# Set-up of a state-space layer: loads reordered, B transposed on TensorE, kernel blocks spread in 2 KB pieces from one queue

## The chip, the cores and the metric

The kernel runs on one core of one Trainium2 chip. A core has TensorE (PE, matrix products and transposes), VectorE (DVE), ScalarE (ACT), GpSimd (POOL) and SyncE (SP, which here only issues DMA transfers), a shared on-chip memory of 128 partitions (SBUF) and an accumulator memory of eight banks (PSUM: ACC has four, SS two, MI two). Engines run on their own and meet at semaphores. The metric is the device time of one execution in microseconds, the median of several.

## The reference

One step of a two-layer decoder over a prompt of 512 tokens and 8 x 4 sample tokens, all in float32. The change lies in the first mixer:

```python
y, h = s5_ssm(rmsnorm(h), ...)      # 64 groups of 16 channels, one 64-dim complex state each
# inside: dt = exp(log_dt); A = exp((lam_re + i lam_im) dt)
#         B' = f(A, lam) * B;  h_t = A h_{t-1} + B' u_t;  y_t = Re(C h_t) + D u_t
gl = gelu(y) @ w_glu + b_glu        # then ConvFFN, embedding gate, attention layer, ConvFFN ...
```

## The kernel before

Nearly all of the time goes to streamed weights: strips of 128 columns of every weight matrix are loaded by SP into RAW, split by GpSimd into two parts (L616, L618) and multiplied by PE (L831). Ahead of the first strip stands the state-space layer, some 200 us, and the change is all in there.

The scan runs in chunks of CH = 8 positions, for 32 pairs of groups. Its set-up, by engine:

- SP (from L426) issues small loads: constants, lam, log_dt, the gain row G2; then B (L439, two transfers straight into BC in the order needed, 64 bytes a piece), C (L443, 16 transfers), vectors, states, convolution parameters. ACT's queue loads x at once (L1239 to L1245).
- PE turns lam and log_dt (L676), makes the gain row in SS (L679), turns C into ACC (L683, `c_made`), turns x by eighths through the two banks of MI (L694), then vectors, convolution parameters, states, and the scaled x (`uz_made`).
- DVE computes the powers of A from log_dt (L1700 to L1816, `a_ready`, `powers_in`), multiplies B by the gains (L1822), builds the powers A^j B for both halves of the pairs (L1843 to L1851, `pc_ready`), makes the diagonal DG (L1855), then the squarings for the rotation table (L1859, "levels", 30 small instructions), the table EROT (L1870), and then one scan for each f of 8 (L1887).
- GpSimd multiplies C by powers in `powers(0)`, as soon as `a_ready` and `c_turned` are there, and `powers(1)` after `uz_made`. Each runs eight half-cycles of two L585 and one L588, on 1, 2, 4 and 1 positions.
- ACT copies C (`c_turned`), squares x (L1255), takes the root (L1258), copies x out of PSUM (L1262), scales it (L1279) and copies results of PE.

The local part of y is a block-Toeplitz product. `kernels(h)` on PE makes its 8 blocks of 16 rows for half h of the pairs, ACT copies them into KKE behind seven blocks of zeros (L1312), and then SP "spreads" them: 64 transfers for each half, one for each of 8 row blocks j and 8 groups b, copy KKE shifted by j blocks into KT (L486), semaphore `kt_in0` or `kt_in1`. PE's `outputs(f)` reads KT (L788); outputs(0) to (3) need the first half, outputs(4) to (7) the second. In PE's program the order is inputs(f + 1), turn_z(f - 1), kernels(1) at f = 1, outputs(f). After both halves SP loads the first weight strip (L491).

Of the kernel before, what the change touches and what calls it, by code (L numbers as in the profile page):

```python
# [18 lines left out]
F32 = mybir.dt.float32  # L19
# [112 lines left out]
def build(nc, x_prompt, x_sample, state_ssm_re, state_ssm_im, state_ffn_conv, cache_k_win, cache_v_win,  # L132
# [5 lines left out]
    with ExitStack() as ctx:  # L138
# [79 lines left out]
        early = Region(n_at + 2 * PAIRS * CH * CG * 4)  # L218
        TAB = early("TAB", [P, 2, 1024])

        KKE = early("KKE", [P, KC // 2, (2 * CH - 1) * CG])
        SSQ = early("SSQ", [P, CH])
        RST = early("RST", [P, CH])
        MSK = early("MSK", [P, CG])
# [13 lines left out]

        Z = nc.alloc_sbuf_tensor_at("Z", [P, KC, 2, NTOK], F32R, offset=perm.at)
        XS = nc.alloc_sbuf_tensor_at("XS", [P, CH, D], F32, offset=perm.at)  # L240
        KT = nc.alloc_sbuf_tensor_at("KT", [P, NBL, P], F32, offset=perm.at + 2048)

        BD = nc.alloc_sbuf_tensor_at("BD", [P, 2, PAIRS, 2 * CG], F32, offset=perm.at + 2048 + NBL * P * 2)
        ph1 = Region(perm.at + 2 * KC * NTOK * 4)
        uz_at = ph1.at
        UZ = ph1("UZ", [P, NBL, NC_])
# [19 lines left out]
        LD2 = stg("LD2", [2, PAIRS])  # L266
        SEL = stg("SEL", [2, P])
        G2 = stg("G2", [2, PAIRS * CG])
        SQJ = stg("SQJ", [P, D])
        assert stg.at <= uz_at + NBL * NC_ * 4  # L270

# [154 lines left out]
        def _(sp):  # L426
            LOAD = [sem("load0"), sem("load1")]

            with nc.allow_non_contiguous_dma(reason="64 small elements"):
# [5 lines left out]
                sp.dma_start(LD2[:], ssm_log_dt[0].rearrange("(q a) -> a q", a=2)).then_inc(sem("lam_in"), 16)  # L435
                sp.dma_start(G2[:].rearrange("a (q c) -> a q c", c=CG),
                             g_mix[0].rearrange("(q a c) -> a q c", a=2, c=CG)).then_inc(sem("g_in"), 16)
            for r, src in enumerate((ssm_b_re, ssm_b_im)):
                sp.dma_start(BC[:, r], src[0].rearrange("(q a) s c -> (a s) q c", a=2)).then_inc(sem("b_in"), 16)  # L439
            for r, src in enumerate((ssm_c_re, ssm_c_im)):  # L440
                for t in range(4):
                    for a in range(2):
                        sp.dma_start(CS_[:, r, t, 64 * a:64 * a + 64],  # L443
                                     src[0].rearrange("(t q a) c s -> t a q c s", t=4, a=2)[t, a]).then_inc(sem("c_in"), 16)
            for at0, src in ((V_GMIX, g_mix), (V_GFFN, g_ffn), (V_GPLE, g_ple)):
                sp.dma_start(VECS[at0:at0 + 16, :], src.rearrange("l (c p) -> (l c) p", p=P)).then_inc(sem("vec_in"), 16)
            sp.dma_start(VECS[V_GKV:V_GKV + 8, :], g_kv.rearrange("(c p) -> c p", p=P)).then_inc(sem("vec_in"), 16)
# [19 lines left out]
            def stream(name, parts, begin=0):  # L467

                def turn(i, free):
                    for u in range(2):  # L470
                        if free:

                            sp.wait_ge(sem("split_done"), i * 2 + (strip_of(name, u) - 1))
                        todo = parts(i, u)
                        for dst, src in todo:
                            sp.dma_start(dst, src).then_inc(LOAD[u], 64 // len(todo))

                n = dict(order)[name] // 2
                if name == "glu":

                    for h in range(2):
                        sp.wait_ge(sem("uz_made"), len(XG))
                        sp.wait_ge(sem("kk_ready"), h + 1)
                        for j in range(CH):
                            for b in range(8):
                                sp.dma_start(KT[CG * j:CG * j + CG, NBL // 2 * h:NBL // 2 * h + NBL // 2, :].rearrange(  # L486
                                    "p (f b) n -> p f b n", b=8)[:, :, b, :],
                                    KKE[CG * b:CG * b + CG, :, CG * (CH - 1 - j):CG * (CH - 1 - j) + P]).then_inc(sem("kt_in%d" % h), 16)

                    sp.wait_ge(sem("kt_in1"), 16 * CH * 8)  # L490
# [66 lines left out]
        def _(pool):  # L557
# [11 lines left out]
            PIN.memset(TIC[:], 0.0).then_inc(sem("ones_set"), 1)  # L569

            pool.wait_ge(sem("ones_set"), 1)
            PIN.memset(KKE[:, :, 0:(CH - 1) * CG], 0.0).then_inc(sem("kz_set"), 1)
            pool.wait_ge(sem("kz_set"), 1)

            def powers(h):
# [90 lines left out]
        def _(pe):  # L666
# [14 lines left out]
            for r in range(2):  # L681
                for t in range(4):
                    last = turn(ACC[:, r, P * t:P * t + P], CS_[:, r, t, :], P)  # L683
                last.then_inc(sem("c_made"), 1)

            pe.wait_ge(sem("x_in"), 112)
            pe.wait_ge(sem("xz_set"), 1)
            pe.wait_ge(sem("xs_zero"), 1)
            for m in range(KC):
                for jh in range(2):  # L690
                    if m:
                        pe.wait_ge(sem("x_turned"), 2 * m + jh - 1)
                    for j in range(4):
                        last = turn(MI[:, jh, NC_ * j:NC_ * j + NC_], XS[0:NC_, 4 * jh + j, P * m:P * m + P], NC_)  # L694
                    last.then_inc(sem("x_made"), 1)
            pe.wait_ge(sem("vec_in"), 160)
            pe.wait_ge(sem("c_turned"), 2)
            turn(ACC[:, 0, 0:V_N], VECS[:], V_N).then_inc(sem("vec_made"), 1)
            pe.wait_ge(sem("cp_in"), 128)
            for t in range(4):  # L700
# [74 lines left out]
            def outputs(f):  # L775


                par = f % 2
                pe.wait_ge(sem("kt_in%d" % (f // 4)), 16 * CH * 8)
                if f:  # L780
                    pe.wait_ge(sem("y_taken"), f)
                else:
                    pe.wait_ge(sem("kk_taken"), 1)
                pe.wait_ge(sem("h0_placed"), f + 1)
                pe.wait_ge(sem("h_ready"), f + 1)
                for q in range(FQ):
                    for a in range(2):
                        mm(SS[0:NU_, a, P * q:P * q + P], UZ[:, 8 * f + 2 * q + a, 0:NU_], KT[:, 8 * f + 2 * q + a, :],  # L788
                           start=True, stop=False, skip_group_check=True)
                    for r in range(2):  # L790
                        for a in range(2):
                            rows = slice(64 * a, 64 * a + 64)
                            last = mm(SS[0:NU_, a, P * q:P * q + P], HSV[rows, par, r, q, 0:NU_],  # L793
                                      CA[rows, r, FQ * f + q, 1:CH + 1, :].rearrange("p t c -> p (t c)"),
                                      start=False, stop=r == 1, skip_group_check=True)
                last.then_inc(sem("y_made"), 1)
# [401 lines left out]
        def _(act):  # L1198
# [60 lines left out]
            for m in range(KC):  # L1259
                for jh in range(2):  # L1260
                    act.wait_ge(sem("x_made"), 2 * m + jh + 1)
                    src = MI[:, jh, 0:4 * NC_].rearrange("p (j c) -> p j c", c=NC_)  # L1262
# [43 lines left out]
            def kernels(h, src):  # L1306
# [5 lines left out]
                copy(KKE[:, :, (CH - 1) * CG:], src.rearrange("p (f n) -> p f n", n=P)).then_inc(sem("kk_taken"), 1)  # L1312
# [364 lines left out]
        def _(dve):  # L1677
# [181 lines left out]
            for lv in range(6):  # L1859
                t = TURNS + 3 * lv  # L1860
                w = A4_RE + 2 if lv == 0 else t - 3
                T(PR[:, X4:X4 + 2, :], PR[:, w:w + 2, :], PR[:, w:w + 2, :], M_)
                link(T(pr(X6), pr(w), pr(w + 1), M_))
                T(pr(t), pr(X4), pr(X5), S_)
                T(pr(t + 2), pr(X4), pr(X5), S_)
                link(T(pr(t + 1), pr(X6), pr(X6), A_))
# [377 lines left out]
```

## Time and profile before

| | |
|---|---|
| median of 3 runs | 1491.46 us (1490.61 to 1493.36) |
| profiled execution, its own time | 1493.79 us |
| its span | 1491.9 us |
| PE busy | 1347.7 us, 90% |
| GpSimd busy | 773.2 us, 52% |
| DVE busy | 752.4 us, 50% |
| ACT busy | 441.6 us, 30% |

```profile
PE   0463769999999999999999998899999999999998
...
PEclk9995779999999999999999999999999999999999
DMA  7011115322222233333355312132332223332322
```

Each of the 40 digits stands for a fortieth of the span, 37.3 us: the busy share in tenths for PE and the DMA engines, the granted TensorE clock in tenths of full speed between them. The first six slices are the set-up; after them PE is busy without a break.

### The profile page before, as it was taken

The page shows a single profiled execution, that of the slowest core. Times are in us where ns is not written, and L with a number is a line of the kernel's source. Part 1 is how long each engine was busy: PE and PEld are TensorE (multiplying, and loading weights), DVE is VectorE, ACT ScalarE, POOL GpSimd, SP SyncE. Part 2 cuts the span into 40 slices and gives each one's busy share as a digit, 9 for nine tenths or more (in the row PEclk, how much of TensorE's full clock was granted, in tenths as well). Part 3 has the DMA queues.
Part 4 walks back from the last instruction along what each step waited for, and adds up shares of the span by engine and source line. Part 5 has one row for each costly group of instructions (what it writes and reads, how often), then busy time and mean ns, then how long its engine had stood idle before and what let it go on. Part 6 is the DMA issues. An engine that isn't in the chain of part 4 may idle for free.

```text
span 1491.9 us, 28737 instructions
## 1 busy us (share of the span) xinstructions
PE 1347.7 (90%) x10924; PEld 1295.5 (87%) x10924; DVE 752.4 (50%) x1310; ACT 441.6 (30%) x941; POOL 773.2 (52%) x669
## 2 busy tenths in 40 slices
PE   0463769999999999999999998899999999999998
PEld 0452548999999999999999985699999999999998
DVE  4886633225555555213376876555555555312253
ACT  0751212113343333111124137423334333210021
POOL 1770005655665556556565545455566655656552
PEclk9995779999999999999999999999999999999999
DMA  7011115322222233333355312132332223332322
GB/s 95 13 22 36 41 47 115 87 84 84 86 84 84 87 93 98 86 91 89 98 113 133 94 43 79 31 95 71 91 92 84 84 84 91 106 90 81 91 86 63
DMA packets 237799, 120.19 MB, mean 81 GB/s; under 512 B 34413, under 2 KB 236992, under 8 KB 237420
## 3 DMA queue, kind: packets, MB, share of 16 engines
q1 hardware_dynamic: 227640, 107.06, 26.1%
q10 hardware_dynamic: 10092, 12.20, 3.9%
q8 instruction: 47, 0.77, 0.2%
q14 instruction: 20, 0.16, 0.0%
HBM read 110.98 MB, written 6.09 MB: 78 GB/s over the span
## 4 chain that ended last, share of the span: by engine, by line
PE 82%; SPq 7%; ACT 4%; DVE 3%; issue 2%; POOL 1%; ACTq 0%; DMA 0%; DVEq 0%; POOLq 0%
PE ACC L831 55%; PE MI L831 10%; PE SS L831 8%; SPq L486 5%; PE MI L671 4%; SPq L439 1%; PE SS L788 1%; PE SS L793 1%; SPq L443 1%; ACT PB L1630 1%; ACT XN L1202 1%; PE SS L1016 1%; PE SS L1138 1%; DVE PB L2173 1%; DVE RSTD L1971 0%
## 5 line engine op out<-in xcount | busy, mean ns | idle before, releaser
L618 POOL TENSOR_TENSOR SPL<-RAW,SPL 128x1024 fp32r<-128x1024 f32 (+2 forms) x172 | 449.6, 2614 | 14.3
L831 PE MATMUL ACC<-NH,SPL 128*128 128x272 f32 x2048 | 350.1, 289 | 0.7 <-DVE AL L2032 0.7
L615 POOL TENSOR_TENSOR TIC<-EPSB 128x1 f32<-128x1 f32 x172 | 37.0, 215 | 597.0 <-PE ACC L831 343.6
L831 PEld LDWEIGHTS ACC<-NH,SPL 128*128 128x128 f32 x2048 | 291.5, 189 | 1.8 <-issue 0.9
L831 PE MATMUL ACC<-AH,SPL 128*128 128x272 f32 x1408 | 237.6, 289 | 0.0
L831 PE MATMUL ACC<-NL,SPL 128*128 128x272 f32 x1024 | 211.3, 288 | 0.0
L831 PEld LDWEIGHTS ACC<-AH,SPL 128*128 128x128 f32 x1408 | 198.9, 188 | 0.2
L616 POOL TENSOR_SCALAR SPL<-RAW 128x1024 fp32r<-128x1024 f32 (+2 forms) x172 | 195.2, 1135 | 0.0
L831 PEld LDWEIGHTS ACC<-NL,SPL 128*128 128x128 f32 x1024 | 160.9, 189 | 0.0
L831 PE MATMUL ACC<-AL,SPL 128*128 128x272 f32 x704 | 145.4, 287 | 0.0
L831 PE MATMUL SS<-NH,SPL 128*128 128x272 f32 x704 | 120.6, 288 | 0.0
L831 PE MATMUL MI<-NH,SPL 128*128 128x272 f32 x704 | 120.6, 288 | 0.0
L1685 DVE SCALAR_TENSOR_TENSOR ACC<-WK,CP,ACC 128x560 f32<-128x560 f32 x88 | 70.9, 805 | 95.7 <-ACT ACC L1202 89.3
L831 PEld LDWEIGHTS ACC<-AL,SPL 128*128 128x128 f32 x704 | 111.0, 188 | 0.0
L2047 DVE TENSOR_TENSOR H<-ACC,H 128x544 f32 (+1 forms) x24 | 17.4, 724 | 183.4 <-PE ACC L831 183.2
L1685 DVE SCALAR_TENSOR_TENSOR NL<-H,VEC,NH (+1 forms) x40 | 80.3, 2016 | 47.7 <-ACT NH L1489 29.7
L831 PE MATMUL ACC<-Z,SPL 128*128 128x272 f32 x768 | 100.0, 292 | 3.2 <-ACT WK L1401 2.3
L831 PEld LDWEIGHTS ACC<-Z,SPL 128*128 128x128 f32 x768 | 98.3, 191 | 4.5 <-issue 3.3
L831 PEld LDWEIGHTS MI<-NH,SPL 128*128 128x128 f32 x704 | 100.5, 189 | 0.0
L831 PEld LDWEIGHTS SS<-NH,SPL 128*128 128x128 f32 x704 | 100.5, 189 | 0.0
L831 PE MATMUL ACC<-XQH,SPL 128*128 128x272 f32 x512 | 90.1, 294 | 0.9 <-DVE XQL L1685 0.9
L831 PEld LDWEIGHTS ACC<-XQH,SPL 128*128 128x128 f32 x512 | 74.4, 191 | 1.9 <-DVE XQL L1685 1.1
(329 smaller groups left out, 2006.2 us busy)
## 6 DMA issues: line engine op xcount, KB each, us to landing
RAW<-in_w_up_dram SPq DMA_DIRECT2D x88, 512.0 KB
RAW<-in_w_down_dram SPq DMA_DIRECT2D x32, 704.0 KB
RAW<-in_w_glu_dram SPq DMA_DIRECT2D x16, 512.0 KB
RAW<-in_w_ple_gate_dram SPq DMA_DIRECT2D x16, 512.0 KB
KT<-KKE SPq DMA_DIRECT2D x128, 32.0 KB, 2.0
RAW<-in_w_q_dram SPq DMA_DIRECT2D x16, 256.0 KB
RAW<-in_w_o_dram SPq DMA_DIRECT2D x32, 128.0 KB
RAW<-in_w_ple_in_dram SPq DMA_DIRECT2D x16, 128.0 KB
```

The lines of the kernel that those rows point to most:

```text
L439: sp.dma_start(BC[:, r], src[0].rearrange("(q a) s c -> (a s) q c", a=2)).then_inc(sem("b_in"), 16)
L443: sp.dma_start(CS_[:, r, t, 64 * a:64 * a + 64], src[0].rearrange("(t q a) c s -> t a q c s", t=4, a=2)[t, a]).then_inc(sem("c_in"), 16)
L486: sp.dma_start(KT[CG * j:CG * j + CG, NBL // 2 * h:NBL // 2 * h + NBL // 2, :].rearrange("p (f b) n -> p f b n", b=8)[:, :, b, :], KKE[CG ...
L615: PIN.tensor_tensor(TIC[:], EPSB[:], EPSB[:], ALU.add)
L616: PIN.tensor_scalar(hi, RAW[:, u, 0:kt, :], 1.0, 1.0, ALU.mult, ALU.mult).then_inc(sem("high_done"), 1)
L618: PIN.tensor_tensor(lo, RAW[:, u, 0:kt, :], hi.bitcast(F32), ALU.subtract).then_inc(sem("split_done"), 1)
L671: return tr(out, in_, IDN[0:rows, 0:rows])
L788: mm(SS[0:NU_, a, P * q:P * q + P], UZ[:, 8 * f + 2 * q + a, 0:NU_], KT[:, 8 * f + 2 * q + a, :], start=True, stop=False, skip_group_check ...
L793: last = mm(SS[0:NU_, a, P * q:P * q + P], HSV[rows, par, r, q, 0:NU_], CA[rows, r, FQ * f + q, 1:CH + 1, :].rearrange("p t c -> p (t c)") ...
L831: last = mm(out[:, h, :], SPL[:, u, w, w0 + k, :], x[:, k0 + k, HT * h:HT * h + HT], start=start and k == 0 and n == 0, stop=stop and k == ...
L1685: return nc.vector.scalar_tensor_tensor(out=out, in0=in0, scalar=scalar, in1=in1, op0=op0, op1=op1)
L2047: T(halves(H[:, i * 2 + u, :]), acc(u), halves(H[:, i * 2 + u, :]), A_).then_inc(sem(norm + "_h"), 1)
```

## The change

The C loads go ahead of the B loads. B comes in its natural order, 8 KB a row, and PE turns it (32 transposes) into ACC; ACT copies the gain row from PSUM to GS first, and DVE's multiplication reads these two. ACT waits for lam and log_dt before it issues the x loads. x is turned through four banks instead of two, and vectors, convolution parameters and states are turned after the last of x is copied. DVE's level loop moves from behind DG to before the multiplication of B. KKE and KT are laid out with the tap (position) outermost, so that one transfer copies 16 rows of 2 KB, contiguous on both sides; there are 128 transfers as before and all are on SP's queue. KT becomes two tensors; the second lies where the first half of PC lies, so SP waits for `v_made` of 4 before it spreads the second half.

```diff
-        KKE = early("KKE", [P, KC // 2, (2 * CH - 1) * CG])
+        KKE = early("KKE", [P, 2 * CH - 1, KC // 2, CG])
...
-        KT = nc.alloc_sbuf_tensor_at("KT", [P, NBL, P], F32, offset=perm.at + 2048)
+        KT = [nc.alloc_sbuf_tensor_at("KT%d" % h, [P, 8, CH, KC // 2, CG], F32, offset=o) for h, o in
+              ((0, perm.at + KC * NTOK * 4), (1, n_at))]
+        BN = nc.alloc_sbuf_tensor_at("BN", [PAIRS, 2, P, CG], F32, offset=n_at)
...
+        XB = (MI[:, 0], MI[:, 1], ACC[:, 0], ACC[:, 1])
+        def spread(h, j, b):
+            return (KT[h][CG * j:CG * j + CG, b].rearrange("p i f c -> p (i f c)"),
+                    KKE[CG * b:CG * b + CG, CH - 1 - j:2 * CH - 1 - j].rearrange("p t f c -> p (t f c)"))
...
-            for r, src in enumerate((ssm_b_re, ssm_b_im)):
-                sp.dma_start(BC[:, r], src[0].rearrange("(q a) s c -> (a s) q c", a=2)).then_inc(sem("b_in"), 16)
             for r, src in enumerate((ssm_c_re, ssm_c_im)):
...
+            for r, src in enumerate((ssm_b_re, ssm_b_im)):
+                sp.dma_start(BN[:, r], src[0].rearrange("(q a) s c -> q (a s) c", a=2)).then_inc(sem("b_in"), 16)
...
                         sp.wait_ge(sem("kk_ready"), h + 1)
+                        if h:
+                            sp.wait_ge(sem("v_made"), KC // 2)
                         for j in range(CH):
                             for b in range(8):
-                                sp.dma_start(KT[CG * j:CG * j + CG, NBL // 2 * h:NBL // 2 * h + NBL // 2, :].rearrange(
-                                    "p (f b) n -> p f b n", b=8)[:, :, b, :],
-                                    KKE[CG * b:CG * b + CG, :, CG * (CH - 1 - j):CG * (CH - 1 - j) + P]).then_inc(sem("kt_in%d" % h), 16)
+                                sp.dma_start(*spread(h, j, b)).then_inc(sem("kt_in%d" % h), 16)
...
+            pe.wait_ge(sem("b_in"), 32)
+            for r in range(2):
+                for c in range(CG):
+                    last = tr(ACC[:, 2 + r, PAIRS * c:PAIRS * c + PAIRS], BN[:, r, :, c], IDN[0:PAIRS, 0:PAIRS])
+            last.then_inc(sem("b_made"), 1)
...
-                    if m:
-                        pe.wait_ge(sem("x_turned"), 2 * m + jh - 1)
+                    if m >= 2:
+                        pe.wait_ge(sem("x_turned"), 2 * m + jh - 3)
...
-            pe.wait_ge(sem("c_turned"), 2)
+            pe.wait_ge(sem("x_turned"), 2 * KC)
             turn(ACC[:, 0, 0:V_N], VECS[:], V_N).then_inc(sem("vec_made"), 1)
...
-                        mm(SS[0:NU_, a, P * q:P * q + P], UZ[:, 8 * f + 2 * q + a, 0:NU_], KT[:, 8 * f + 2 * q + a, :],
+                        mm(SS[0:NU_, a, P * q:P * q + P], UZ[:, 8 * f + 2 * q + a, 0:NU_], KT[f // 4][:, 2 * q + a, :, f % 4, :],
...
+            act.wait_ge(sem("lam_in"), 48)
             for i in range(4):
                 act.dma_start(XS[NSEQ:64, 2 * i:2 * i + 2, :], chunks[0:64 - NSEQ, 2 * i:2 * i + 2, :]).then_inc(sem("x_in"), 16)
...
+            act.wait_ge(sem("g_made"), 1)
+            copy(GS[:], SS[:, 1, :]).then_inc(sem("g_copied"), 1)
...
-            dve.wait_ge(sem("g_made"), 1)
-            dve.wait_ge(sem("b_in"), 32)
+
+            for lv in range(6):
+                t = TURNS + 3 * lv
...
+            dve.wait_ge(sem("g_copied"), 1)
+            dve.wait_ge(sem("b_made"), 1)
             for r in range(2):
-                last = T(BC[:, r].rearrange("p q c -> p (q c)"), BC[:, r].rearrange("p q c -> p (q c)"), SS[:, 1, :], M_)
+                last = T(BC[:, r], ACC[:, 2 + r, :].rearrange("p (c q) -> p q c", q=PAIRS), GS[:].rearrange("p (q c) -> p q c", c=CG), M_)
```

## Rows read from the trace of the kernel before

**Rows 1.** The page's chain that ended last, shares by engine

```profile
PE 82%; SPq 7%; ACT 4%; DVE 3%; issue 2%; POOL 1%; ACTq 0%; DMA 0%; DVEq 0%; POOLq 0%
```

**Rows 2.** Chain in order of time, 0 to 260 us: start, us, what

```profile
4.26 19.23 SPq L439
```

**Rows 3.** Source line L486, SP: ns min/median/max, first and last start

```profile
L486 SPq DMA_DIRECT2D KT<-KKE x128: 585/595/1572, 95.3 to 197.2; - x128
...
DMA to landing us min/median/max: 2.0/2.0/3.1
```

**Rows 4.** Timeline 0 to 60 us: start, us, engine, line, operation [idle before]

```profile
2.95 0.32 SPq L435 DMA_DIRECT2D LD<-in_ssm_log_dt_dram  x1
...
23.04 0.34 PE L671 MATMUL SS<-IDN,LAMS 64*128 64x64 f32 x1 [23.04 <-DMA LD<-in_ssm_log_dt_dram]
...
38.62 0.35 DVE L1816 COPY SS<-PR 128x192 f32<-128x192 f32 x1
...
39.01 1.28 DVE L1822 TENSOR_TENSOR BC<-BC,SS 128x512 f32<-128x512 f32 x2
...
39.55 1.05 ACT L1255 ACTIVATE ZTK<-XS 80x1024 f32<-80x1024 f32 x1
...
49.73 0.20 DVE L1845 RECIPROCAL RST<-RST 80x8 f32<-80x8 f32 x1 [5.33 <-ACT RST L1258]
```

**Rows 5.** Timeline 57 to 100 us

```profile
76.33 1.22 DVE L1834 TENSOR_TENSOR PC<-TE,ACC 128x1024 f32<-128x1024 f32 x1
...
83.12 0.29 DVE L1857 TENSOR_TENSOR DG<-MSK,DGV 128x128 f32<-128x128 f32 x1
...
87.95 0.65 PEld L751 LDWEIGHTS SS<-CA,BD 128*32 128x32 f32 x16 [0.33 <-issue]
...
94.36 0.60 ACT L1202 ACTIVATE KKE<-SS 128x512 f32<-128x512 f32 x1 [5.70 <-PE SS L754]
...
95.28 5.29 SPq L486 DMA_DIRECT2D KT<-KKE  x8
```

**Rows 6.** Timeline 57 to 170 us, DVE beside GpSimd

```profile
93.92 1.32 POOL L588 TENSOR_TENSOR CA<-TAB 128x512 f32<-128x512 f32 x1
...
94.03 1.26 DVE L1865 TENSOR_TENSOR PR<-PR 128x32 f32<-128x32 f32 x1
...
95.33 3.76 POOL L585 TENSOR_TENSOR TAB<-CA,PR 128x1024 f32<-128x1024 f32 x2
...
99.17 2.41 POOL L588 TENSOR_TENSOR CA<-TAB 128x1024 f32<-128x1024 f32 x1
...
101.83 0.09 DVE L1868 MEMSET EROT<- 128x32 f32 x1
```

**Rows 7.** DMA queues, 7-8 and 18-19 us: packets, MB, engine share

```profile
q10 hardware_dynamic: 28, 0.19, 87.0%
...
q1 hardware_dynamic: 98, 0.01, 60.7%
```

**Rows 8.** Issues by source line: ns min/median/max; timeline on SP

```profile
L539 SPq DMA_DIRECT2D RAW<-in_w_o_dram x8: 596/617/718, 868.8 to 877.8; - x8
...
37.50 0.32 SPq L449 DMA_DIRECT2D VECS<-in_b_glu_dram  x1
...
37.86 0.56 SPq L452 DMA_DIRECT2D VECS<-in_k_norm_dram  x2
```

**Rows 9.** Timeline 100 to 262 us

```profile
124.42 0.08 DVE L1883 MEMSET HSV<- 128x8 f32 x2
...
138.52 1.12 PE L788 MATMUL SS<-KT,UZ 128*72 128x128 f32 x4 [10.38 <-DMA KT<-KKE]
...
154.20 0.60 ACT L1202 ACTIVATE KKE<-ACC 128x512 f32<-128x512 f32 x1 [4.53 <-PE ACC L754]
...
161.55 1.22 PE L770 MATMUL ACC<-UZ,PC 128*64 128x72 f32 x32
...
199.22 1.13 PE L788 MATMUL SS<-KT,UZ 128*72 128x128 f32 x4 [22.46 <-DMA KT<-KKE]
```

More of the change, by code:

```diff
@@ L240, in build @@
         XS = nc.alloc_sbuf_tensor_at("XS", [P, CH, D], F32, offset=perm.at)
-        KT = nc.alloc_sbuf_tensor_at("KT", [P, NBL, P], F32, offset=perm.at + 2048)
-        BD = nc.alloc_sbuf_tensor_at("BD", [P, 2, PAIRS, 2 * CG], F32, offset=perm.at + 2048 + NBL * P * 2)
+        KT = [nc.alloc_sbuf_tensor_at("KT%d" % h, [P, 8, CH, KC // 2, CG], F32, offset=o) for h, o in
+              ((0, perm.at + KC * NTOK * 4), (1, n_at))]
+        BD = nc.alloc_sbuf_tensor_at("BD", [P, 2, PAIRS, 2 * CG], F32, offset=perm.at + KC * NTOK * 4 - 8192)
+        BN = nc.alloc_sbuf_tensor_at("BN", [PAIRS, 2, P, CG], F32, offset=n_at)
         ph1 = Region(perm.at + 2 * KC * NTOK * 4)
@@ L268, in build @@
         G2 = stg("G2", [2, PAIRS * CG])
+        GS = stg("GS", [P, PAIRS * CG])
         SQJ = stg("SQJ", [P, D])
@@ L571, in _ @@
             pool.wait_ge(sem("ones_set"), 1)
-            PIN.memset(KKE[:, :, 0:(CH - 1) * CG], 0.0).then_inc(sem("kz_set"), 1)
+            PIN.memset(KKE[:, 0:CH - 1], 0.0).then_inc(sem("kz_set"), 1)
             pool.wait_ge(sem("kz_set"), 1)
@@ L688, in _ @@
             pe.wait_ge(sem("xs_zero"), 1)
+            pe.wait_ge(sem("c_turned"), 2)
             for m in range(KC):
                 for jh in range(2):
-                    if m:
-                        pe.wait_ge(sem("x_turned"), 2 * m + jh - 1)
+                    if m >= 2:
+                        pe.wait_ge(sem("x_turned"), 2 * m + jh - 3)
                     for j in range(4):
-                        last = turn(MI[:, jh, NC_ * j:NC_ * j + NC_], XS[0:NC_, 4 * jh + j, P * m:P * m + P], NC_)
+                        last = turn(XB[2 * (m % 2) + jh][:, NC_ * j:NC_ * j + NC_], XS[0:NC_, 4 * jh + j, P * m:P * m + P], NC_)
                     last.then_inc(sem("x_made"), 1)
             pe.wait_ge(sem("vec_in"), 160)
-            pe.wait_ge(sem("c_turned"), 2)
+            pe.wait_ge(sem("x_turned"), 2 * KC)
             turn(ACC[:, 0, 0:V_N], VECS[:], V_N).then_inc(sem("vec_made"), 1)
@@ L1261, in _ @@
                     act.wait_ge(sem("x_made"), 2 * m + jh + 1)
-                    src = MI[:, jh, 0:4 * NC_].rearrange("p (j c) -> p j c", c=NC_)
+                    src = XB[2 * (m % 2) + jh][:, 0:4 * NC_].rearrange("p (j c) -> p j c", c=NC_)
                     if jh == 0:
@@ L1311, in kernels @@
                 act.wait_ge(sem("kz_set"), 1)
-                copy(KKE[:, :, (CH - 1) * CG:], src.rearrange("p (f n) -> p f n", n=P)).then_inc(sem("kk_taken"), 1)
+                copy(KKE[:, CH - 1:].rearrange("p t f c -> p f t c"), src.rearrange("p (f t c) -> p f t c", f=KC // 2, c=CG)).then_inc(sem("kk_taken"), 1)
                 act.wait_ge(sem("kk_taken"), h + 1)
@@ L1818, in _ @@
             dve.wait_ge(sem("powers_in"), 1)
-            dve.wait_ge(sem("g_made"), 1)
-            dve.wait_ge(sem("b_in"), 32)
+            for lv in range(6):
+                t = TURNS + 3 * lv
+                w = A4_RE + 2 if lv == 0 else t - 3
+                T(PR[:, X4:X4 + 2, :], PR[:, w:w + 2, :], PR[:, w:w + 2, :], M_)
+                link(T(pr(X6), pr(w), pr(w + 1), M_))
+                T(pr(t), pr(X4), pr(X5), S_)
+                T(pr(t + 2), pr(X4), pr(X5), S_)
+                link(T(pr(t + 1), pr(X6), pr(X6), A_))
+            dve.wait_ge(sem("g_copied"), 1)
+            dve.wait_ge(sem("b_made"), 1)
             for r in range(2):
-                last = T(BC[:, r].rearrange("p q c -> p (q c)"), BC[:, r].rearrange("p q c -> p (q c)"), SS[:, 1, :], M_)
+                last = T(BC[:, r], ACC[:, 2 + r, :].rearrange("p (c q) -> p q c", q=PAIRS), GS[:].rearrange("p (q c) -> p q c", c=CG), M_)
             link(last)
@@ L1857, in _ @@
             T(DG[:], MSK[:].unsqueeze(1).to_broadcast([P, KC, CG]), DGV[:].unsqueeze(2).to_broadcast([P, KC, CG]), M_).then_inc(sem("dg_ready"), 1)
[L1859 to L1866, printed above, removed]
             dve.wait_ge(sem("uz_made"), len(XG))
```

## The prediction

> **What bounds the kernel now.** The page's chain by engine comes first: TensorE holds 82% of it, SyncE's queue 7% [rows 1]. The 7% is where this change acts. The chain in order of time puts it in two places: a 19.2 us issue of the second B load at 4.26 [rows 2], and the "spreading" transfers. There are 128 of them, median 0.595 us to issue, 2.0 us to land [rows 3]. Before the weight strips can stream, the kernel is a chain of set-up, and its steps are these. PE starts at 23.04 on log_dt, issued at 2.95; DVE computes the powers, done at 38.97 (38.62 + 0.35), 15.9 us later; ACT squares x from 39.55; DVE idles 5.33 us for the root at 49.73 [rows 4]. DVE ends the B powers at 77.55, makes DG at 83.12, PE starts kernels(0) at 87.95, ACT copies it at 94.36, SP spreads from 95.28 [rows 5]. PE's outputs(0) starts at 138.52 when the last transfer lands, and outputs(4) at 199.22 after a 22.46 us wait for the second half [rows 9]. Everything behind outputs(4) only shifts with it: the work from there on is unchanged.
>
> **Loads and log_dt.** The change holds the x loads until lam_in. Where is log_dt then? Before, the x queue filled 87% of the DMA engines (7 to 8 us), and even at 18 to 19 us SP's queue moved 98 packets in 60.7% of 16 engine-us, 99 ns a packet [rows 7]. Alone, log_dt's 64 four-byte pieces cost 3 to 6 us at that price. Issue end 3.27, plus 2.0 to land, plus 3.0: 8.3. Bounds are 5.3 (pieces free) and 23.0 (x had no part in it); I take 8.3, as the queue ahead of it holds only small loads. Powers then end at 24.2.
>
> The Trainium skill ("DMA: Bandwidth & Descriptors", on why a DMA increments its semaphore by 16) says that a transfer from SP or ACT uses the largest number of engines up to 16 that divides the slowest dimension of both sides. For log_dt that is 2, so 32 pieces each: an estimate of 3.2 us at the row's 99 ns, landing at 8.5; on one engine 6.3 us and 11.6. No row shows single engines; either would shift the sum by at most 3 us.
>
> x then lands at about 24.6 (before, x ran some 16.3 us from its first issue: the x queue's packets end by 17 us in the DMA view) plus up to 5 for C and B beside it; I take 27.5. ACT starts squaring there instead of 39.55, 12 us sooner. The x transposes through four banks are worth some 2 us, the vec, conv and state transposes now queued behind them cost 1. So the ACT/PE chain would reach kernels(0) 13 us sooner, at 75. B in 8 KB rows frees SP of the 19.2 us issue; its 32 PE transposes (under 0.2 us each) and one ACT copy lie inside that wait for x.
>
> **The moved level loop.** DVE's 30 instructions for the rotation levels move from after DG to before B is multiplied. In the old place they were slow: a step of DVE on 32 columns ends with the step of GpSimd beside it, L1865 at 94.03 + 1.26 = 95.29 and POOL L588 at 93.92 + 1.32 = 95.24. So levels advance one per GpSimd half-cycle (two L585, one L588): from DG's end at 83.41 to 101.83 it is 18.4 us [rows 5, 6], of which the first level, before GpSimd started, 0.8. Six levels at that 0.8 are some 5 us. In the new place GpSimd's powers(0) starts as soon as C is turned. C is now first in the queue, and I put C turned at 19 to 29, centre 23. That is beside the loop at 24.2. The five levels that met GpSimd took 17.6; a sixth meets a second half-cycle of the longest kind, 3.76 + 2.41 = 6.2 [rows 6]. That is 24 us, so B is multiplied at 48.3, not 29: nine later than before. From there to the end of the B powers is 77.55 - 39.01 - 5.33 (the wait for the root is gone by then) = 33.2 [rows 4, 5], giving 81.5. DG 0.5 more. kernels(0) needs DG and DVE works in order: it starts at 82.1 instead of 75. Net against before: **-5.8 us**. Bounds: -13 (no collision) and 0.
>
> The Trainium skill ("SBUF — State Buffer", section "SBUF: two separate sides") speaks against this move: a VectorE instruction with two SBUF inputs and a GpSimd instruction that reads SBUF exclude each other for whole instructions, while one with a PSUM input does not contend. The trace agrees, 1.26 beside 1.32 us. By that rule the whole loop costs 24 us if powers(0) runs through it; without it the sum is that of the first rival below.
>
> The rotation table (101.8 to 124.4, 22.6 us [rows 6, 9]) then starts at 82.1, beside powers(1); 24 us, and the first scan 5.7 us: 112. That is below the next figure, so it is hidden. If the spread were 4 us shorter still, it would be next.
>
> **Spreading.** Before: 95.28 to 138.52 is 43.2 us = 64 x 0.644 + 2.0; second half, from about 155.1 (ACT's copy into KKE at 154.20 plus 0.9) to 199.22, 44.1 = 64 x 0.658 + 2.0 [rows 5, 9]. Each transfer was 64 pieces of 512 B, a stepped pattern on both sides. It becomes 16 contiguous pieces of 2 KB. Price of such an issue: nearest is b_glu, 16 rows against 16 rows, 0.316 us, next issue 0.36 after it. Against it stands 0.617 for w_o's issues, whose pattern is stepped again [rows 8]. I take 0.33 + 0.05 = 0.38, since the plain two-level pattern is what b_glu has. Then a half is 64 x 0.38 + 2.0 = 26.3: **-16.9** and **-17.8**. Bounds 0.30 and 0.67 per transfer. The transferred bytes stay; DMA is no limit.
>
> **The new wait.** SP now waits before the second half until inputs(3) is done on PE, as KT[1] lies on PC. PE finished it at 161.55 + 1.22 = 162.8, SP had started at 155.1: **+7.7** [rows 9]. Behind the wait on SP are only the 64 transfers and then the first glu strips. PE's outputs(1) to (3) run meanwhile. The strided KT operand (64 B runs) and the strided KKE copy (0.60 us, twice) I take at nothing, as the same columns pass. The bounds: four L788 took 1.12 us [rows 9], and 96 of the 128 lie on the path (outputs 2 and 3 do not), so a fifth more each is 5 us, double 27.
>
> **Sum.** -5.8 - 16.9 + 7.7 - 17.8 = -32.8. In steps: SP starts at 89.4, outputs(0) at 115.7, second spread at 140.0, outputs(4) at 166.4 instead of 199.2. Against the profiled execution, 1493.8 us with a span of 1491.9, that is 1461.0; it lies 2.3 over the median of 1491.46, so the median becomes 1458.7.
>
> **Rivals.**
> (a) No collision: C lands late enough, or log_dt early enough, that the levels end first. kernels(0) at 75, sum -13 - 34.7 + 7.7 = -40.0: 1451.5. For it: x fills the engines while C lands. Against: C is issued first.
> (b) log_dt stays late at 23.0, by its own small pieces: powers at 38.9, plus 24 + 33.2 + 0.6 puts kernels(0) at 96.7, +8.7. Sum -18.3: 1473.2. For it: 99 ns packets with x gone.
> (c) Slower: an issue costs by transfer, not by piece. W_o's issues took as long as the spreading ones with other pieces. At 0.617 + 0.05 each of the 128 costs 0.667 against 0.651: nothing comes back, +2.0, and the new wait's 7.7 outweighs the 5.8: +3.9, 1495.4. It decides from about 0.636 per transfer.
> (d) The strided operand slows PE by a fifth: 1464.
>
> **Numbers.** Main 0.48, own range 1451 to 1470; (a), with partial collisions, 0.24; (b) 0.14; (c) 0.07; (d) and others 0.07. The range of 8 in 10 reaches 1444 to 1477. A measurement tells about 0.2%, 3 us, from nothing. Faster 0.90, same 0.04, slower 0.06.
>
> **What would show it.** PE's first matmul near 8 us; ACT L1255's counterpart near 27; the level loop 20 us or more long with GpSimd busy beside it; DVE and not PE late for kernels(0); issues of 0.33; SP idle some 8 us for v_made after the second kernels; outputs(4) near 166. An issue of 0.59 makes the prediction wrong by itself; so does a first matmul at 20.

## The result, and the profile after

The changed kernel takes 1489.4 us (median of 16, 1485.8 to 1491.6) beside 1492.2 (16 runs, 1489.7 to 1496.6) for the kernel before: ratio 0.9974, interval 0.9963 to 0.9984. It is faster by 0.16 to 0.37%, where 2.2% were forecast, and lies outside the range. The profiled execution, 1488.0 us with a span of 1486.0, is 5.9 below the span before; the medians differ by 2.8, so of the last 3 us of any accounting here nothing is sure. Each variant below was run beside the kernel before. Where two variants are compared, both the difference of the medians and that of the two ratios are given if they disagree.

The steps of the prediction, in us on the profiled timelines:

| step | before | predicted | after |
|---|---|---|---|
| PE starts on log_dt | 23.04 | 8.3 | 4.89 |
| powers done on DVE | 38.97 | 24.2 | 20.84 |
| six levels take | (behind DG) 18.4 | 24 | 4.7 |
| ACT squares x | 39.55 | 27.5 | 31.73 |
| DG | 83.12 | 81.5 | 73.21 |
| kernels(0) | 87.95 | 82.1 | 78.05 |
| SP spreads, first half | 95.28 | 89.4 | 83.42 |
| outputs(0) | 138.52 | 115.7 | 126.69 |
| SP spreads, second half | 155.10 | 140.0 | 150.76 |
| outputs(4) | 199.22 | 166.4 | 193.20 |

The page's chain by engine has hardly moved; SyncE's queue still has its 7% [rows 1]:

```profile
PE 83%; SPq 7%; ACT 4%; DVE 3%; issue 2%; POOL 1%; ACTq 0%; DMA 0%; DVEq 0%; POOLq 0%
```

The source line of the spreading transfers says why: with 2 KB pieces in place of 512 B ones, the issue has the price that it had [rows 3], and so has the landing.

```profile
L498 SPq DMA_DIRECT2D KT<-KKE x128: 507/589/1702, 83.4 to 191.2; - x128
...
DMA to landing us min/median/max: 1.9/2.0/3.1
```

The timeline of the changed kernel from 0 to 40 us (start, us, engine, line, operation) shows the loads. PE's wait for log_dt ends at 4.89. DVE runs the first level at 20.87 and ends the sixth at 25.57, while GpSimd is idle until 31.53. PE waits 21.11 us for the last C load and turns C; ACT copies it out before it squares x [rows 4]:

```profile
4.89 0.34 PE L681 MATMUL SS<-IDN,LAMS 64*128 64x64 f32 x1 [4.89 <-DMA LD<-in_ssm_log_dt_dram]
...
9.12 17.95 SPq L451 DMA_DIRECT2D CSTG<-in_ssm_c_im_dram  x8
...
20.49 0.35 DVE L1837 COPY SS<-PR 128x192 f32<-128x192 f32 x1
20.87 0.22 DVE L1844 TENSOR_TENSOR PR<-PR 128x64 f32<-128x64 f32 x1
...
25.39 0.18 DVE L1848 TENSOR_TENSOR PR<-PR 128x32 f32<-128x32 f32 x1
...
28.76 1.97 PE L681 MATMUL ACC<-IDN,CSTG 128*128 128x128 f32 x8 [21.11 <-DMA CSTG<-in_ssm_c_im_dram]
...
31.53 1.20 POOL L595 TENSOR_TENSOR TAB<-CA,PR 128x256 f32<-128x256 f32 x2 [25.36 <-ACT CA L1219]
31.73 1.05 ACT L1276 ACTIVATE ZTK<-XS 80x1024 f32<-80x1024 f32 x1
...
35.51 1.29 DVE L1852 TENSOR_TENSOR BC<-ACC,GS 128x512 f32<-128x512 f32 x2 [9.94 <-PE ACC L699]
```

Farther on the same timeline (60 to 200 us): kernels(0) at 78.05, whose first group runs at 1.10 us for 16 matmuls and the other three at 0.67, where all four took 1.10 before; the two bursts; outputs(0) and outputs(4) held by the transfers [rows 5, 9].

```profile
73.21 0.29 DVE L1887 TENSOR_TENSOR DG<-MSK,DGV 128x128 f32<-128x128 f32 x1
...
78.05 1.10 PE L768 MATMUL SS<-CA,BD 128*32 128x128 f32 x16
79.62 0.67 PE L768 MATMUL SS<-CA,BD 128*32 128x128 f32 x16
...
82.50 0.60 ACT L1219 ACTIVATE KKE<-SS 128x512 f32<-128x512 f32 x1 [3.75 <-PE SS L771]
83.42 6.96 SPq L498 DMA_DIRECT2D KT<-KKE  x11
...
126.69 1.12 PE L805 MATMUL SS<-KT,UZ 128*72 128x128 f32 x4 [25.59 <-DMA KT<-KKE]
...
142.42 0.60 ACT L1219 ACTIVATE KKE<-ACC 128x512 f32<-128x512 f32 x1 [4.89 <-PE ACC L771]
143.05 0.20 ACT L1335 ACTIVATE TIC<-EPSB 128x1 f32<-128x1 f32 x1
149.44 1.22 PE L787 MATMUL ACC<-UZ,PC 128*64 128x72 f32 x32
150.76 14.50 SPq L498 DMA_DIRECT2D KT<-KKE  x22
...
193.20 1.13 PE L805 MATMUL SS<-KT,UZ 128*72 128x128 f32 x4 [28.55 <-DMA KT<-KKE]
```

So: -11.9 at the first spreading start, nothing in the first burst (43.27 against 43.24), +7.5 for the new wait (143.25, when ACT's signal is out, to 150.76), -1.7 in the second burst (42.44 against 44.12). Before rounding the sum is -6.0, which is outputs(4)'s shift (199.22 to 193.20); the span's is 5.9. From outputs(4) to the end all profiled kernels take the same time, 1292.0 to 1294.6 us.

The faster groups of kernels(0), 2.0 of the 11.9, can't be put down to the change. Two of the kernels below, both with few transfers, are the same program up to that point. One ran its last groups at 0.67 and the other at 1.10 (timelines of 80 to 160 us, the first line from the run with eight loads a half, the second from the one with the store early):

```profile
81.29 0.67 PE L771 MATMUL SS<-CA,BD 128*32 128x128 f32 x16
...
82.47 1.10 PE L771 MATMUL SS<-CA,BD 128*32 128x128 f32 x16
```

So this pace can differ between executions of the same instructions. The granted clock doesn't explain it here: from 80 to 83 us it reads 1.00 in the changed kernel, whose groups run at 0.67, and 1.00 in the variant with the levels behind DG, whose groups run at 1.10. Why is open.

### The profile page after: what moved, and what is told of

It reads as the page before. It is cut to its first block, busy times and chain, and to the rows that moved or that the text cites. A ratio compares the mean times of both kernels' runs of the same rounds, so it can differ in the third digit from the quotient of the medians.

```text
span 1486.0 us, 28802 instructions
## 1 busy us (share of the span) xinstructions
PE 1346.1 (91%) x10956; PEld 1295.6 (87%) x10956; DVE 746.7 (50%) x1310; ACT 441.7 (30%) x942; POOL 780.0 (52%) x669
## 4 chain that ended last, share of the span: by engine, by line
PE 83%; SPq 7%; ACT 4%; DVE 3%; issue 2%; POOL 1%; ACTq 0%; DMA 0%; DVEq 0%; POOLq 0%
PE ACC L848 55%; PE MI L848 10%; PE SS L848 8%; SPq L498 5%; PE MI L681 3%; SPq L451 1%; PE SS L810 1%; PE SS L805 1%; ACT PB L1651 1%; ACT XN L1219 1%; PE SS L1033 1%; PE ACC L681 1%; PE SS L1155 1%; DVE PB L2194 1%; DVE RSTD L1992 0%
## 5 line engine op out<-in xcount | busy, mean ns | idle before, releaser
L628 POOL TENSOR_TENSOR SPL<-RAW,SPL 128x1024 fp32r<-128x1024 f32 (+2 forms) x172 | 449.8, 2615 | 14.4
```

Of the source, the lines that this page charges most:

```text
L628: PIN.tensor_tensor(lo, RAW[:, u, 0:kt, :], hi.bitcast(F32), ALU.subtract).then_inc(sem("split_done"), 1)
```

## Experiments

**Prices of single transfers.** SP's queue issues bursts of 24 transfers of different kinds between two SBUF buffers or DRAM, each burst alone.

```
+ sp.dma_start(B[16 partitions, 512 floats], A[16 partitions, 512 floats])       # L45
+ sp.dma_start(B[16 partitions, 4 x 128 floats], A[16 partitions, 4 x 128 floats, stepped])   # L50: 4 pieces of 512 B a row
+ sp.dma_start(B[...], src[16:32, 512 floats])   # L55: DRAM to SBUF
+ sp.dma_start(spare[...], A[...])               # L60: SBUF to DRAM
+ 1 x 2 KB (L75); 16 x 64 B (L80); 16 rows of 16 KB (L95); two queues at once (L100 on SP, L110 on ACT)
```

> This kernel computes nothing of the reference: SP issues bursts of 24 transfers of one form each, and waits for the landings between bursts. It asks what the 0.59 us that each spreading transfer keeps SP (before and after the change) hangs on. Theory A, a price by transfer whatever it carries, in a long burst: every burst shows a median of 0.59, the 1-row, 4-row, 8-row, 16 x 64 B and 128 x 2 KB ones too. Theory B, the price of the on-chip source with on-chip destination: 0.59 in the SBUF to SBUF bursts, 0.30 to 0.40 in the bursts of 16 x 2 KB from or to DRAM. Theory C, by pieces or bytes: 1 row and 16 x 64 B well under 0.4, 128 rows above 0.59. Theory D, by the stepped pattern, on which my prediction stood: 4 x 512 B a row 0.59, 2 KB a row 0.33; the changed kernel's trace speaks against it already. The last burst runs on SP and ACT at once: if both keep 0.59 a second queue doubles the rate; if each goes to 1.2 the two share one generator.

Measured (source line views: ns min/median/max, first and last start):

```profile
L45 SPq DMA_DIRECT2D B<-A x24: 563/589/590, 18.0 to 32.5; - x24
...
L50 SPq DMA_DIRECT2D B<-A x24: 594/595/672, 34.4 to 49.2; - x24
...
L55 SPq DMA_DIRECT2D B<-in_src_dram x24: 403/420/423, 51.2 to 61.8; - x24
...
L60 SPq DMA_DIRECT2D spare<-A x24: 302/420/478, 63.6 to 74.5; - x24
...
L75 SPq DMA_DIRECT2D B<-A x24: 583/589/590, 110.0 to 124.5; - x24
...
L80 SPq DMA_DIRECT2D B<-A x24: 531/589/591, 126.2 to 140.7; - x24
...
L95 SPq DMA_DIRECT2D B<-A x8: 572/2518/2691, 164.7 to 178.2; - x8
...
L100 SPq DMA_DIRECT2D B<-A x24: 507/590/607, 187.5 to 202.1; - x24
...
L110 ACTq DMA_DIRECT2D C<-A x24: 555/611/766, 187.6 to 202.4; - x24
```

A transfer from SBUF to SBUF costs 0.589 us to issue whether it is one piece of 2 KB, 16 of 2 KB or 16 of 64 B. With four pieces of 512 B a row, the form that the change replaced, it costs 0.595. With DRAM on either side, 16 plain rows cost 0.42. So the pieces were not what cost, and b_glu's 0.316, which the prediction took, is a load from DRAM. Even that was no price for a burst: the 24 DRAM loads of L55 start 0.46 us apart. The ends are not the whole rule either, as a DRAM load can cost as much by its shape: the median stepped C load of the changed kernel takes 0.589, and w_o's 0.617 [rows 8]. Two queues at once keep their rate: 48 transfers in 15.4 us.

**The loads and the levels alone.** The changed kernel with the old KKE and KT layout, 512 B pieces and no wait for v_made.

```
- sp.wait_ge(sem("v_made"), KC // 2)
- sp.dma_start(*spread(h, j, b))
+ sp.dma_start(KT[CG*j:CG*j+CG, ...][:, :, b, :], KKE[CG*b:CG*b+CG, :, CG*(CH-1-j):CG*(CH-1-j)+P])
```

> The changed kernel with KT, KKE, the spreading transfers and the missing v_made wait of the kernel before: the load order, B on TensorE and the moved level loop alone. My theory (the loads gave 11.9 us at the start of the first spread, the wait took 7.5 back, the pieces nothing): spread starts near 83.4, outputs(0) near 126.7, second spread right after kk_ready near 143, outputs(4) near 187; time 11 to 13 us under before, 0.992 of it, and 5 to 7 under the changed kernel. Rival (2 KB pieces do help somewhere, in landing or contention): not faster than the changed kernel, 0.997.

Measured 1483.75 us, ratio 0.9942 (0.9929 to 0.9956). The spread starts at 83.39, outputs(0) at 126.97, and the second half's transfers at 143.50, as soon as ACT's signal is out. Outputs(4) starts 5.5 before the changed kernel's (timeline of 110 to 200 us):

```profile
187.68 1.13 PE L803 MATMUL SS<-KT,UZ 128*72 128x128 f32 x4 [23.03 <-DMA KT<-KKE]
```

By its ratio this half of the change is worth 8.6 us (6.6 to 10.6). The steps came as expected and the time did not: 11 to 13 were forecast, from a timeline that had the 2.0 of kernels(0)'s faster groups in it.

**The pieces alone.** The kernel before with the new layout, 2 KB pieces and the wait, the loads and the levels as they were.

```
- KKE = early("KKE", [P, KC // 2, (2 * CH - 1) * CG])
+ KKE = early("KKE", [P, 2 * CH - 1, KC // 2, CG])
+ if h: sp.wait_ge(sem("v_made"), KC // 2)
+ sp.dma_start(*spread(h, j, b))
```

> The kernel before with KT and KKE by tap, 2 KB pieces and the v_made wait, the loads and the level loop left as before. My theory: first spread 95.3 to 138 as before at 0.59 an issue, second held from 155 to 162.8, so 6 to 8 us slower than before: 1.004 to 1.005. Rival (the pieces help): same or faster than before. The strided KT operand would show as L788 above 0.28 us at the low clock and 0.16 at the high.

Measured 1499.49 us, ratio 1.005 (1.0036 to 1.0063): 7.5 slower (5.4 to 9.4), as the new wait's price would have it. (Its profiled execution is only 3.1 over the span before, as its spreading started at 92.24.) The two halves together, -8.6 and +7.5, give -1.1 against a measured -3.9 (-5.5 to -2.4), about what their intervals allow. The second burst takes 42.7 here (159.51 to 202.25), 42.4 in the changed kernel, and 44.1 to 44.2 in the two kernels with 512 B pieces. The first bursts differ by less, 42.9 and 43.3 against 43.2 and 43.6. So there may be 1 or 2 us in the pieces; as the second burst also starts behind another wait, no run separates the two.

**Few transfers.** KKE goes to device memory in one store and comes back in 8 loads of 256 KB a half.

```
+ sp.dma_start(kk_rows[h], KKE[:].rearrange("p t f c -> p (t f c)")).then_inc(sem("kd_out"), 16)
+ sp.wait_ge(sem("kd_out"), 16 * (h + 1))
  for j in range(CH):
-     for b in range(8):
-         sp.dma_start(*spread(h, j, b))
+     sp.dma_start(KT[h][CG*j:CG*j+CG].rearrange(...), kk_rows[h].rearrange("(b c) x -> c b x", b=8)[..., 64*(CH-1-j): +512])
```

> The changed kernel with the spreading of a half as one store of KKE to DRAM (480 KB), its landing, and 8 loads of 256 KB (16 rows by 8 pieces of 2 KB) in place of 64 transfers of 32 KB; bytes into KT unchanged. Theory 1, the number of issues is the wall: half lands some 17 us after its start instead of 43; outputs(0) then waits for DVE's first scan (about 110), outputs(4) near 151 instead of 193; time 36 to 44 us under before, 0.972. Theory 2, bytes or the writes of 16 rows are the wall (53 GB/s seen): nothing gained, and the round trip costs 3 to 6 us more than the changed kernel: 1.000.

Measured 1448.2 us (1445.8 to 1452.9), ratio 0.9707 (0.9683 to 0.9731): 41 us below the changed kernel by the medians, 40 by the ratios, and outputs(4) starts 38.8 earlier. Its timeline (80 to 160 us) has the store, the eight loads in 3.6 us, an outputs(0) that now waits for DVE's scan, and an outputs(4) that waits 7 us where it waited 28.6:

```profile
83.24 0.36 SPq L496 DMA_DIRECT2D kk_rows<-KKE  x1
...
85.80 3.63 SPq L499 DMA_DIRECT2D KT<-kk_rows  x8
...
109.41 1.10 PE L808 MATMUL SS<-KT,UZ 128*72 128x128 f32 x4 [8.85 <-DVE HSV L1934]
...
133.47 0.34 SPq L496 DMA_DIRECT2D kk_rows<-KKE  x1
...
154.40 1.13 PE L808 MATMUL SS<-KT,UZ 128*72 128x128 f32 x4 [7.04 <-DMA KT<-kk_rows]
```

The bytes and the pieces that go into KT are the same as in the changed kernel. What changed is the number of issues, 9 for 64, and that each now has one end in DRAM. This run doesn't separate the two. By an estimate, 64 issues 0.46 apart, as in the DRAM burst of the single prices, and 2.0 to land would be 31.4 us; the burst takes 43.3, and this run's second half 20.9 (133.47 to 154.40). So the ends alone could give 11.9 and leave 10.5 to the number. That it is SP's issuing and not the way between the two ends that fills the 43 us is shown by the next run, which leaves both ends in SBUF. What is left here is the transfers themselves: from 135 to 150 us the DMA engines are busy by 0.84 and more, where the spreading held them at 0.20 to 0.25. Still fewer issues should gain little; that was not run.

**Two queues.** The changed kernel, blocks 4 to 7 of the first half issued by ACT behind its KKE copy.

```
-     for b in range(8):                      # SP
+     for b in range(4 if h == 0 else 8):
...
+ act.wait_ge(sem("kk_ready"), 1)
+ act.wait_ge(sem("uz_made"), len(XG))
+ for j in range(CH):
+     for b in range(4, 8):
+         act.dma_start(*spread(0, j, b)).then_inc(sem("kt_in0"), 16)
```

> The changed kernel, but half of the first half's spreading (blocks 4 to 7 of each tap, 32 of the 64 transfers) is issued by ScalarE behind its copy of the kernels; the second half stays on SyncE. Theory 1 (the price of a spreading transfer is its issue on one queue, 0.64 us, and two queues don't share it, as in the run of single prices): the first half's transfers are out 0.64 x 32 = 20.5 us after the start instead of 41, so the first outputs matmul comes at about 107 to 110 instead of 126.7, bounded by VectorE's scan (ready near 109.8); v_made follows sooner by as much, the second burst starts near 135 instead of 150.8, the fifth outputs group near 177 instead of 193.2: 1489.4 - 16 = 1473 us (1468 to 1479). ScalarE is held for some 20 us, its turned copies of the next input groups come late by that, which is a cost that the idle 25 us of TensorE hide. Theory 2 (the price is paid in what both queues share: descriptor generation for a transfer with both ends on chip, or the 16 engines): both queues slow to about 1.2 us a transfer, the first outputs matmul stays at 126 or later, 1489 to 1495 us.

Measured 1471.8 us, ratio 0.9872 (0.9858 to 0.9886), 1.2 from the forecast. That is 17.6 below the changed kernel by the medians and 15.2 by the ratios; outputs(4) starts 14.4 earlier. The timeline of 80 to 120 us:

```profile
85.57 20.82 ACTq L1341 DMA_DIRECT2D KT<-KKE  x32
85.63 21.04 SPq L498 DMA_DIRECT2D KT<-KKE  x32
...
106.44 0.32 ACT L1219 ACTIVATE VSM<-ACC 128x32 f32<-128x32 f32 x2 [20.89 <-issue]
...
106.89 1.29 DVE L1922 TENSOR_TENSOR T<-ACC,EROT 128x512 f32<-128x512 f32 x2 [9.20 <-ACT VSM L1219]
```

Both queues issue at 0.65 us each side by side: half the transfers, half the time. Not all is as forecast: ACT, held for 20.9 us, copies the samples late, DVE's scan waits 9.2 for that, and outputs(0) starts at about 118, not at 107 to 110. Outputs(4) starts at 178.8 instead of 193.2. The Trainium skill ("DMA: Bandwidth & Descriptors", section "Issuing engines are not separate DMA queues") says that a second issuing engine saves only the time of initiating, "usually small relative to the DMA itself". The saving is as it says; it isn't small here: 0.65 of issue for each transfer in the queue against one landing of 2.0 at the end. The Trainium skill ("Perfetto Trace Analysis", section "DMA Instruction — HWDGE (DVE, Sync)") has one descriptor generator shared by two sequencers, each locking it for itself while its descriptors are made. If that took up most of an issue, the two bursts would take nearly twice as long; with 0.590 and 0.611 side by side against 0.589 alone, no run shows such a wait.

**The x loads not held.**

```
- act.wait_ge(sem("lam_in"), 48)
```

> The changed kernel, but ScalarE's loads of x do not wait for the lambda and log_dt loads to land. Theory 1 (the x transfers filling the engines are what kept log_dt at 23 us in the kernel before): log_dt lands late again, near 20 to 23 us instead of 4.9; powers and levels then end near 43 instead of 25.6; x lands some 4 us sooner and the C loads no later than 28.7; the B multiply that starts at 35.5 moves to 44 or later, so all up to the spreading start moves 6 to 10 us later (83.4 to 90 to 93): 1489.4 + 8 = 1497 us (1493 to 1501). Theory 2 (it is the loads' order on SyncE's queue and the missing B loads that let log_dt land early, the wait does nothing): within 1 us of the changed kernel, 1488 to 1491 us.

Measured 1507.1 us, ratio 1.0105 (1.0089 to 1.012): 17.7 above the changed kernel by the medians, 19.5 by the ratios: twice the forecast of 8. The direction holds, as PE gets log_dt only at 21.57. The size is the collision of the prediction, which comes true here. C is turned before the powers end, GpSimd's powers(0) runs, and the six levels take from 40.26 to 62.37, 22.1 us for 4.7. These are PE's first line (timeline of 0 to 45 us) and then DVE and GpSimd on the timeline of 36 to 64 us:

```profile
21.57 0.34 PE L681 MATMUL SS<-IDN,LAMS 64*128 64x64 f32 x1 [21.57 <-DMA LD<-in_ssm_log_dt_dram]
...
40.26 0.23 DVE L1843 TENSOR_TENSOR PR<-PR 128x64 f32<-128x64 f32 x1
40.37 2.05 POOL L595 TENSOR_TENSOR TAB<-CA,PR 128x512 f32<-128x512 f32 x2 [2.31 <-DVE SS L1836]
...
51.25 2.43 POOL L598 TENSOR_TENSOR CA<-TAB 128x1024 f32<-128x1024 f32 x1
51.26 0.23 DVE L1843 TENSOR_TENSOR PR<-PR 128x64 f32<-128x64 f32 x1
51.40 2.33 DVE L1844 TENSOR_TENSOR PR<-PR 128x32 f32<-128x32 f32 x1
...
62.40 1.29 DVE L1851 TENSOR_TENSOR BC<-ACC,GS 128x512 f32<-128x512 f32 x2
```

The step of 2.33 beside GpSimd's 2.43 takes 0.18 alone. Spreading starts at 104.3 instead of 83.4.

**The levels behind DG again.** The rest as in the changed kernel.

```
- for lv in range(6): ...        # ahead of the B multiply
+ for lv in range(6): ...        # the same five instructions each, behind DG
```

> The changed kernel, but the loop of six levels stands again behind the gather of DG on VectorE. Theory 1 (the levels fall in idle time of VectorE at 20.9 to 25.6 us, 4.7 us in all, so moving them gained nothing for the spreading's start, and behind DG they delay only the rotation tables, whose scan is done 17 us before the first outputs matmul needs it): spreading starts at 83.4 as in the changed kernel, the levels collide with GpSimd and take 12 to 25 us there, the first scan is ready at 122 to 135 instead of 109.8; the first outputs matmul waits for the spread (126.7) or for the scan up to 8 us beyond: 1489.4 to 1497 us, forecast 1491. Theory 2 (the early levels are what let the first kernels come sooner, since something on their way reads them): spreading starts later than 86 and the time goes to 1493 or more by the start alone.

Measured 1489.4 us, ratio 0.9988 (0.9978 to 0.9998), beside the changed kernel's 0.9974. The levels take 18.4 us behind DG (73.41 to 91.82) and nobody waits: kernels(0) still starts at 78.04. Spreading starts at 85.4, not 83.4: all four groups of kernels(0) ran at 1.10 us here, the later three at 0.67 in the changed kernel, and no step of the levels lies between. This is the last of them (timeline of 60 to 110 us):

```profile
82.76 1.10 PE L768 MATMUL SS<-CA,BD 128*32 128x128 f32 x16
```

As said above, this pace differs between executions. So no gain of the moved loop is seen with these loads: the medians are equal and the two intervals overlap. Where x is not held, the loop meets powers(0) and its place matters; the run without the hold shows the collision, though not what the old place would have given there.

**The x loads held until C has landed.**

```
- act.wait_ge(sem("lam_in"), 48)
+ act.wait_ge(sem("c_in"), 256)
```

> The changed kernel, but ScalarE's loads of x wait until all 16 C loads have landed, instead of the lambda and log_dt loads. Theory 1 (what stretches the C issues to 18 us for eight is the x transfers in flight, 2.36 MB on the same 16 engines): the 16 C issues take 0.6 us each as in the second group of the run without the hold (5.01 us for eight), C lands near 16 instead of 28.7 and its turn is done near 19; x starts at 16 and lands 13 us or so later, near 29 to 31, so ScalarE's squares start at 29 to 31 instead of 31.8, and the spreading starts 0 to 3 us sooner than 83.4: 1488 us (1485 to 1491). Theory 2 (C issues are slow by their own stepped shape, 256 B pieces over 32 partitions): C lands no sooner than 22 even without x, x then lands at 35 or later, and the spreading starts 4 us or more later: 1493 us or more.

Measured 1495.8 us, ratio 1.0015 (1.0006 to 1.0025), some 6 above the changed kernel, where 1488 was forecast. My theory 1 had the mechanism and not the end. The C issues take 10.2 us for 16 (5.22 + 5.01), and C is in at 16.2 instead of 28.7: it was the x transfers that stretched them. But x, first issued at 16.17, is in at 38.13, after 22 us, not 13. In the timeline of 0 to 40 us:

```profile
3.63 5.22 SPq L451 DMA_DIRECT2D CSTG<-in_ssm_c_re_dram  x8
...
8.90 5.01 SPq L451 DMA_DIRECT2D CSTG<-in_ssm_c_im_dram  x8
...
16.17 1.92 ACTq L1260 DMA_DIRECT2D XS<-in_x_prompt_dram  x4
...
38.13 1.06 ACT L1276 ACTIVATE ZTK<-XS 80x1024 f32<-80x1024 f32 x1 [16.01 <-DMA XS<-in_x_prompt_dram]
```

Spreading starts at 91.8. The overlap of x and C in the changed kernel is worth more than either alone: both are in by 31.7.

**Two variants of the few transfers.** The store of the second half ahead of SP's wait for v_made (only the loads overwrite what is waited for), and that with x held until C is in.

```
  sp.wait_ge(sem("kk_ready"), h + 1)
- if h: sp.wait_ge(sem("v_made"), KC // 2)
  sp.dma_start(kk_rows[h], KKE ...)
  sp.wait_ge(sem("kd_out"), 16 * (h + 1))
+ if h: sp.wait_ge(sem("v_made"), KC // 2)
```

> The kernel with KKE stored to device memory and read back by 8 loads a half (1448.2 us), but in the second half the store goes out before SyncE waits for the last of the half's input matmuls (only the loads, which overwrite the place that they read, need that wait). Theory 1 (store and its landing, 0.36 + 2.2 us, stand in the chain behind v_made in the second half): the loads start at the v_made signal (133.5) instead of 136, and the second half's outputs come up to 2.5 us sooner if TensorE waits for them: 1446 us (1444 to 1449). Theory 2 (the second half's outputs wait for VectorE's scan, not for the transfers, once those are few): no change, 1447 to 1450 us.

> The kernel with KKE stored to device memory and read back by 8 loads a half, store ahead of the v_made wait (1448.4 us), with the x loads also held until C has landed. Theory 1: the same 0 to 3 us at the start as in the run beside it; but the end of this stage now hangs on VectorE's scan (ready at 109.4), which depends on the rotation tables beside GpSimd, not on x; so of the 0 to 3 us only part arrives: 1447 us (1444 to 1450). Theory 2: 1452 us or more, as the later x shifts all of the half's inputs.

Measured 1448.4 us (1445.2 to 1451.9), ratio 0.9723 (0.9709 to 0.9738), and 1453.6, ratio 0.973 (0.9708 to 0.9751). Neither is faster than the 1448.2. In the profile of the first one outputs(4) starts at 148.66 against 154.40, and 3.4 of that comes from an earlier v_made (130.03 against 133.47), which the edit doesn't touch: kernels(1) happened to run at the faster pace. With four runs each, 7 us apart, the other 2.5 us can't be told. In the second one the forecast of 1447 failed and its rival came true, as all comes later with x: the first store starts at 89.72 instead of 83.24, and outputs(4) at 157.55. The best kernel found is the one with 8 loads a half, 3% below both.

## Why the prediction was wrong

**Spreading: the failed step.** "I take 0.33 + 0.05 = 0.38, since the plain two-level pattern is what b_glu has". Spacing stayed at 0.63 to 0.65. This is the whole miss and more: -34.7 predicted, -1.7 measured, 33.0 short, of which some 6 came back in the steps before it. The rows held two prices, and I chose by the count of dimensions. For a transfer with both ends in SBUF that count made no difference (0.595 and 0.589), and b_glu comes from DRAM. The transfers at hand, SBUF to SBUF, had their own price in [rows 3]; nothing in the trace showed a cheaper one of their kind. Rival (c) had it ("an issue costs by transfer, not by piece"), at a chance of 0.07, with a spacing of 0.667 for the measured 0.63 to 0.65. Its evidence, w_o's 0.617, agreed only by its size, being a DRAM load too; what the single prices add is that an SBUF to SBUF issue is at 0.58 to 0.62 in every small shape tried. That 64 issues are the wall of each half was right: fewer gave some -40 us, two queues for one half some -15.

**Loads and log_dt: right, and more.** Holding x lets log_dt land at 4.9 (8.3 predicted); rival (b) fell, and without the hold log_dt is at 21.6. The 3 us that I charged for its pieces were not there. Powers 20.8 for 24.2. ACT squares at 31.7 for 27.5: not for x, whose queue has no packet after 26 us in the DMA view, but for C, whose turn ACT copies first. C landed at 28.7 and GpSimd could start on it at 31.5, later than my 19 to 29 for C turned, because three of SP's last eight C issues took 3.2 to 6.8 us each while x filled the engines. I had charged x with C's traffic, and not C's issues with x's.

**The moved level loop: the condition failed, not the price.** 24 us were predicted for a loop beside powers(0); 22.1 were measured when the two met (x not held), 4.7 when they did not. In the changed kernel the levels end at 25.57 and powers(0) starts at 31.53, so rival (a) came true in this step, by its condition that the levels end first: kernels(0) at 78.05, between its 75 and my 82.1. The Trainium skill's rule ("SBUF — State Buffer", "SBUF: two separate sides"), cited there against the move, holds as a mechanism by 0.18 against 2.33 us for one step; whether it costs is a question of when C lands. The term came out at -9.9 instead of -5.8. The spreading start is at -11.9, and the 2.0 between them, kernels(0)'s faster groups, can't be put down to the change.

**The new wait: right.** 7.7 predicted, 7.5 measured; the pieces alone were 7.5 slower. That it fits to 0.2 is partly luck, as the wait lasts as long as PE needs for outputs(1) to (3): with two queues, where these ran at the faster pace, it was 5.0 (131.15 to 136.15).

**Rival (d): refuted.** Four strided matmuls take 1.12 us as before.

**Sum.** With the measured terms, -9.9 - 2.0 + 7.5 - 1.7 = -6.1: rival (c)'s price with rival (a)'s loads. Without the 2.0 it is -4.1, beside the -3.9 that the ratio gives. I had priced each rival with the rest as in the main case, so no case held this pair. Rival (c)'s 1495.4 would have read 1488 with (a)'s -13 in place of the -5.8.

## To carry to other kernels

Before a burst of small transfers is reshaped, ask for the price of one issue of the same kind, with both its ends in the same memories; if the spacing of the burst equals it, expect help from fewer transfers or a second queue, as here, and not from larger pieces. A loop that collides with another engine is priced by its condition: find out when the other engine can start, from the load that releases it. And where rivals concern different steps, work out their pairs too.

## What was not expected of the hardware

- Issuing SBUF to SBUF takes 0.58 to 0.62 us for 1 to 128 rows and pieces of 64 B to 2 KB; the plain 16 rows from DRAM or to it take 0.42, the stepped C loads from DRAM 0.59. Only 16 rows of 16 KB took 2.5.
- SP and ACT issue side by side with hardly any slowing: 0.590 and 0.611 us, against 0.589 alone.
- Issues stall on another queue's traffic: eight C issues took 17.95 us beside the x loads and 5.01 without them.
- Going to device memory and back (2.5 us to land a 0.49 MB store, then 2 MB in some 18 us) beats 64 direct transfers of the same data, 43 us.
- The same 16 matmuls took 0.67 us in one execution and 1.10 in another, at a granted clock of 1.00 in both.
